# Forgetting attention: the row-maximum pass multiplies rounded copies of queries and keys

## The reference, cut to what matters

```python
q = rmsnorm(q.reshape(B, Lp, ATT_HEADS, ATT_HEAD_DIM), q_gain).transpose(0, 2, 1, 3)
k = rmsnorm(k.reshape(B, Lp, ATT_HEADS, ATT_HEAD_DIM), k_gain).transpose(0, 2, 1, 3)
logf = jax.nn.log_sigmoid(fl.astype(jnp.float32) + b_forget.astype(jnp.float32))
c = jnp.cumsum(logf, axis=1).transpose(0, 2, 1)
...
s = jnp.einsum('bhqd,bhkd->bhqk', q_i, k).astype(jnp.float32) * scale
s = s + c_i[..., :, None] - c[:, :, None, :]
mask = (pos[None, :] <= p_i[:, None]) & (pos[None, :] >= pad)
p = jax.nn.softmax(jnp.where(mask, s, NEG), axis=-1)
return jnp.einsum('bhqk,bhkd->bqhd', p.astype(v.dtype), v)
```

## Time and profile before

| | us |
|---|---|
| median of 3 runs | 2737.48 |
| lowest, highest | 2736.27, 2741.62 |
| span of the profiled execution | 2732.2 |
| TensorE busy in it | 2546.3 (93%) |
| VectorE, ScalarE, GpSimd busy | 1369.3, 973.2, 985.7 |
| forgetting attention, pairs 0 to 7 | from about 950 to 1300 |

### The profile page before, as it was taken

How to read it: one execution, slowest core, us unless ns; L and a number is a source line. 1 busy time by engine, 2 the same in 40 slices (tenths; PEclk the granted TensorE clock), 3 DMA queues, 4 the chain that set the end, 5 groups by cost and what they waited for, 6 DMA issues and landing times.

```text
span 2732.2 us, 45723 instructions
## 1 busy us (share of the span) xinstructions
PE 2546.3 (93%) x19794; PEld 2286.5 (84%) x19794; DVE 1369.3 (50%) x2057; ACT 973.2 (36%) x1565; POOL 985.7 (36%) x585
## 2 busy tenths in 40 slices
PE   7989978799999999999999999989998979999997
PEld 5877767678888888887999999988988968999997
DVE  4634455462635354444264554466654534727363
ACT  5234344232323444334433332354332224333232
POOL 1743344544444322222434444500002214445444
PEclk9999999999999999999999999999999988999998
DMA  9432120333332221111222332322111012233221
GB/s 248 121 94 63 53 70 24 92 96 97 93 93 87 68 55 47 40 47 40 78 62 85 89 90 85 87 59 70 40 33 36 17 32 59 85 92 87 87 87 60
DMA packets 379927, 201.33 MB, mean 74 GB/s; under 512 B 6464, under 2 KB 377152, under 8 KB 379728
## 3 DMA queue, kind: packets, MB, share of 16 engines
q1 hardware_dynamic: 379728, 198.42, 25.8%
HBM read 196.30 MB, written 2.10 MB: 73 GB/s over the span
## 4 chain that ended last, share of the span: by engine, by line
PE 57%; DVE 22%; ACT 11%; issue 4%; POOL 4%; DMA 1%; POOLq 0%; ACTq 0%; SPq 0%; DVEq 0%
PE ps L645 40%; DVE t_ffy L2829 7%; ACT t_wh L613 5%; DVE t_ffy L2832 2%; ACT t_ffy L2736 2%; DVE t_atq L2628 2%; POOL t_wl L623 1%; PE ps L2436 1%; DVE t_wl L623 1%; DVE t_ffy L2838 1%; PE ps L3061 1%; PE ps L2409 1%; PE ps L2375 1%; PE ps L3080 1%; PE ps L1090 1%
## 5 line engine op out<-in xcount | busy, mean ns | idle before, releaser
L623 POOL TENSOR_TENSOR t_wl<-t_raw,t_wh 128x1024 fp32r<-128x1024 f32 (+2 forms) x268 | 611.1, 2281 | 1030.1 <-ACT t_wh L613 1030.1
L613 ACT ACTIVATE t_wh<-t_raw 128x1024 fp32r<-128x1024 f32 (+2 forms) x323 | 327.7, 1015 | 605.8 <-PE ps L645 562.4
L645 PE MATMUL ps<-t_hh,t_wh 128*128 128x264 f32 (+2 forms) x2048 | 473.4, 310 | 14.4 <-DVE t_dcq L2562 3.6
L645 PE MATMUL ps<-t_hh,t_wl 128*128 128x264 f32 (+2 forms) x2048 | 449.4, 298 | 8.0 <-POOL t_wl L623 4.3
L645 PE MATMUL ps<-t_hl,t_wh 128*128 128x264 f32 (+2 forms) x2048 | 446.0, 299 | 0.0
L645 PEld LDWEIGHTS ps<-t_hh,t_wh 128*128 128x128 f32 x2048 | 323.7, 192 | 36.5 <-issue 17.6
L645 PEld LDWEIGHTS ps<-t_hh,t_wl 128*128 128x128 f32 x2048 | 324.0, 191 | 24.2 <-POOL t_wl L623 6.9
L645 PEld LDWEIGHTS ps<-t_hl,t_wh 128*128 128x128 f32 x2048 | 322.6, 191 | 9.1 <-issue 1.5
L645 PE MATMUL ps<-t_fhh,t_wh 128*128 128x264 f32 (+1 forms) x1040 | 280.9, 324 | 6.5 <-DVE t_fhl L1753 4.9
L645 PE MATMUL ps<-t_fhh,t_wl 128*128 128x264 f32 (+1 forms) x1040 | 281.5, 325 | 4.6 <-POOL t_wl L623 4.5
L2829 DVE SCALAR_TENSOR_TENSOR t_ffy<-t_ffp,t_vec,t_ffy 128x528 f32<-128x528 f32 x88 | 216.8, 2463 | 130.6 <-ACT t_ffy L2736 130.6
(11 more groups left out here) (558 smaller groups left out, 4351.3 us busy)
## 6 DMA issues: line engine op xcount, KB each, us to landing
t_raw<-in_up SPq DMA_DIRECT2D x44, 512.0 KB, 3.8
t_raw<-in_up2a SPq DMA_DIRECT2D x44, 512.0 KB, 3.9
t_raw<-in_up2b SPq DMA_DIRECT2D x44, 512.0 KB, 3.9
t_raw<-in_attn_in SPq DMA_DIRECT2D x33, 512.0 KB, 4.1
t_raw<-in_dn_in SPq DMA_DIRECT2D x33, 512.0 KB, 4.1
t_raw<-in_ada_w SPq DMA_DIRECT2D x32, 512.0 KB, 4.4
t_raw<-in_w_in SPq DMA_DIRECT2D x25, 512.0 KB, 4.4
t_raw<-in_down SPq DMA_DIRECT2D x16, 512.0 KB, 3.8
```

What stands on the lines that cost most here:

```text
L613: ac.activation(wh[slot_of[j]][:, 0:kc, :], raw[r % NRAW][:, 0:kc, :], ACT.Copy).then_inc(up("wh_cut", "cut", j), 1)
L623: eng.tensor_tensor(wl[slot_of[j]][:, 0:kc, :], raw[r % NRAW][:, 0:kc, :], wh[slot_of[j]][:, 0:kc, :].bitcast(F), SUB).then_inc(up(name, " ...
L645: ins = pe.matmul(ps[bank_of(j, i)][:, 0:tn], wt[slot][:, k, :], a[:, k, t0:t0 + tn], start=first, stop=last)
```

## The change

GpSimd gets a new kind of work, `round`: two copies of 128x528, the pair's normed queries and keys, into fp32r tiles (`t_aqr`, `t_akr`). It is put into the plan behind the pair's second `pair_norm`, but not before the pair ahead has put its six `row_max` steps, since the copies have one buffer (pair 0 has its own, in space of `t_apt`; pair 1's share space with `cT` and `aglog` and wait for their last readers). `row_max` multiplies the copies and waits for `rounded`; the wait for both norms moves to `weights`, which still multiplies `aq` and `ak` in fp32.

```diff
-        AFTER["pair_norm"] = lambda use, p, m: ready_qk.add((p, m))
+        rounded_at, maxima = [0], [0]
+
+        def put_round():
+            p = rounded_at[0]
+            if (p, 1) in ready_qk and p <= maxima[0]:
+                put("round", p)
+                rounded_at[0] += 1
+
+        def normed_pair(use, p, m):
+            ready_qk.add((p, m))
+            put_round()
+
+        AFTER["pair_norm"] = normed_pair
...
                     for i in range(6):
                         put("row_max", p, i, banks=2)
                         yield 1
+                    maxima[0] += 1
+                    put_round()
...
-                for m in range(2):
-                    w.wait_ge(s.normed, at("normed", "pair_norm", p, m))
+                w.wait_ge(s.rounded, at("rounded", "round", p))
...
-                    pe.matmul(ps[b][0:tn, 0:wide], aq[p % 3][64 * e:64 * e + 64, t0:t0 + tn],
-                              ak[p % 3][64 * e:64 * e + 64, a:a + wide], start=True, stop=False)
+                    qr, kr = (qround, kround) if p else (qround0, kround0)
+                    pe.matmul(ps[b][0:tn, 0:wide], qr[64 * e:64 * e + 64, t0:t0 + tn],
+                              kr[64 * e:64 * e + 64, a:a + wide], start=True, stop=False)
...
                 w.wait_ge(s.copied, at("copied", "turn_max", p))
+                for m in range(2):
+                    w.wait_ge(s.normed, at("normed", "pair_norm", p, m))
...
+            def round_(p):
+                for m in range(2):
+                    w.wait_ge(s.normed, at("normed", "pair_norm", p, m))
+                if p == 1:
+                    w.wait_ge(s.turned, at("turned", "split_c"))
+                    w.wait_ge(s.lo_dve, at("lo_dve", "split_c"))
+                elif p:
+                    w.wait_ge(s.scored, at("scored", "row_max", p - 1, 5))
+                qr, kr = (qround, kround) if p else (qround0, kround0)
+                po.tensor_copy(qr[:, :], aq[p % 3][:, :])
+                po.tensor_copy(kr[:, :], ak[p % 3][:, :]).then_inc(up("rounded", "round", p), 1)
```

More of the change, by code:

```diff
@@ L111 @@
     "lev_in lo_dve lo_pool mask_in maxed mm_done mod_mm mod_part mod_set multiplied normed out_d pool_step pool_x "
-    "rel_in rooted roped rstd_a rstd_d scaled scored sin_in sp_done sp_in sp_out spread sq_dve sq_pool "
+    "rel_in rooted roped rstd_a rstd_d scaled scored rounded sin_in sp_done sp_in sp_out spread sq_dve sq_pool "
     "squared step_x summed took_a took_d turned vec_in weighed wh_cut wl_dve wl_pool "
@@ L1849, in program @@
         sb_ = ExitStack()
+        with ExitStack() as st:
+            kround = sbt(st, "akr", [128, L], R)
         cT = sbt(sb_, "cT", [16, L])
@@ L1865, in program @@
         mrow = [sbt(sb_, f"amr{i}", [128, L], R) for i in range(2)]
+        with ExitStack() as st:
+            qround0, kround0 = sbt(st, "aqr0", [128, L], R), sbt(st, "akr0", [128, L], R)
         pT = [sbt(sb_, f"apt{i}", [128, 1360]) for i in range(2)]
         inv = sbt(sb_, "ainv", [128, L // 2])
+        with ExitStack() as st:
+            qround = sbt(st, "aqr", [128, L], R)
         glog = sbt(sb_, "aglog", [128, L])
@@ L2032, in program @@
             "pair_norm": "multiplied rooted inverted normed",
-            "values": "turned copied", "row_max": "scored maxed", "turn_max": "turned copied",
+            "values": "turned copied", "round": "rounded", "row_max": "scored maxed", "turn_max": "turned copied",
             "weights": "scored exped", "mixing": "weighed inverted scaled",
@@ L2694, in gated @@
                                  SUB).then_inc(up("lo_pool", "gated", pr), 1)
-            return {"gated": gated}
+            def round_(p):
[9 more added lines that the diff above has]
+                po.tensor_copy(kr[:, :], ak[p % 3][:, :]).then_inc(up("rounded", "round", p), 1)
+            return {"gated": gated, "round": round_}
         def stream_scalar(ac, w):
```

## The result

The changed kernel takes 2748.63 us (median of ten executions, 2741.7 to 2752.47) where the kernel before takes 2736.82 (2733.66 to 2741.73). The ratio is 1.004, 95% interval 1.003 to 1.005: 11.8 us, 0.43%. Timed a second time, in five rounds beside the kernel before (last experiment), it was 1.0039 (1.0024 to 1.0053), with 9.6 us between the medians. So it is slower by more than the 0.2% that can be told from no change.

A forecast was written before the change was run, and what follows sets the result against it. TensorE's columns were taken to bound the attention. Product gain -11.5, stalls +11.75, pair 0 +0.45 and clock +4.35 sum to +5.05 us; added to the median of 2737.48 this gave 2742.5 us, range 2733 to 2750.

The forecast's parts named there:

- Gain of the product: Row-maximum pass on TensorE: fp32r product saves 1.6 us a pair, 0.3 in pair 1, 11.5 us in total.
- Price of a cast: GpSimd's two new 128x528 casts per pair: 0.92 us each, the middle between 0.54 and 1.31.
- The queue and the stall: GpSimd's rounding holds a low half TensorE wants: five stalls of 2.55 us in pairs 3 to 7, 11.75 us lost net.
- 0.71 + 2T: TensorE's stall per pair in pairs 3 to 7, with T the time of one GpSimd cast: 2.55 us.
- T: Time of one 128x528 cast on GpSimd, taken as 0.92 us.
- the collision: Pair 7: VectorE's two-operand gating product slows beside GpSimd's held low halves, so 1.0 us comes back and not 1.43.
- The clock: TensorE's granted clock halves after three of the five stalls, 1.45 us each, 4.35 us in total.
- three drops: Half-clock pieces of about 3.4 us on TensorE after three of five stalls, 1.45 us each: 4.35 us.
- cheap-cast rival: Casts on GpSimd take 0.54 us, stalls 1.79 us, the clock holds: -3.5 us, 2734 us; chance 0.25.
- dear-cast rival: Casts on GpSimd take 1.31 us and the clock falls after every stall: +12.6 us, 2750 us; chance 0.19.
- harmless queue: Low half behind GpSimd's rounding isn't wanted so early, so the gain stays: some -11 us, 2726.5 us; chance 0.1.
- product without gain: Row-maximum product: 64 rows in fp32r run no faster than fp32, only losses stay, some +16.5 us; chance 0.01.

The follow-up runs named there:

- last experiment: The changed kernel, unaltered, timed again in five rounds beside the kernel before: 2745.77 us, ratio 1.0039.
- repeat of the late version: The changed kernel with each pair's rounding planned behind the low half of the panel two on, measured a second time on another chip: 2726.46 us, ratio 0.9968.
- late version: The changed kernel with each pair's rounding planned after the halves of the panel two on, not ahead of them: 2727.0 us, ratio 0.9955.
- pair-1 experiment: The late version with pair 1 alone multiplying its unrounded fp32 queries and keys: 2728.64 us, ratio 0.9958.

## Why the prediction was right, and where it was not

The time (2748.63) lies in the range of 2733 to 2750, near its upper end, and the sign was right; but the forecast said 2742.5, a change within 0.2%, and it is +0.43%. That the time lies in the range is in part luck, since two terms were wrong by several us in opposite directions. By its steps:

**Gain of the product: right.** 1.6 us a pair was forecast; pairs 2 and 6, which have no drop in their passes, are 1.68 us shorter, and the 400-column step takes the 0.55 us forecast. The 0.1 us taken off for exposed weight loads was not needed. For pair 1 I had left 0.3 us, for the same two reasons that the trace shows: the wait before step 4 (the steps counted from 0) grew by 0.85 us and step 5 waits 0.34 us for the same reductions. In the repeat of the late version, where the clock falls only behind this pass, it takes 10.71 us from its first step to its last mask and not 11.10, so the pair keeps 0.4. In all 12.2 us where I had 11.5.

**Price of a cast: wrong, and it helped the change.** I took the middle of 0.54 and 1.31 us, 0.92. It is 0.58 from start to start, close to the memset that only writes. Between two ends that lie far apart the middle had nothing for it. And there was a row of the same work, on another engine: the trace of before has a copy of 128x528 from fp32 into fp32r eight times on ScalarE, at 0.64 us (the line below). The Trainium skill (GPSIMD Engine Reference, Engine selection) had it: one-input operations run at roughly line rate, and the trace agrees with its 0.625 us for 528 columns. Pair 0 therefore cost nothing (0.45 forecast).

```profile
L2536 ACT ACTIVATE t_oh<-t_aog 128x528 fp32r<-128x528 f32 x8 | 5.2, 644 | 8.5 <-DVE t_aog L2665 8.5
```

**The queue and the stall: right in mechanism and place.** Five waits at L645 behind t_wl, in pairs 3 to 7 and nowhere else; with the measured 1.16 us for both casts the formula 0.71 + 2T gives 1.87 us, and 1.64 plus 0.2 of a slower start is 1.84. The late version removes all five, which shows the cause and doesn't only argue it. With T = 0.92 I had 11.75 us of stalls; it is 7.8. Pair 7 gave back its whole 1.43 us and not 1.0. VectorE's gating product in pair 7, beside the held low halves, took 1.27 us and not 1.03: the collision that I took from pair 0's 1.90 us is there, but cost little. In pair 0 itself it is as large as ever, 2.43 us for L1120 beside the low half; and in pair 2 it is the cast that takes 1.11 us instead of 0.62 beside that product, which itself takes 0.71, as good as the 0.70 before:

```profile
1035.95 0.62 POOL L2727 CAST t_aqr<-t_aq 128x528 fp32r<-128x528 f32 x1 [23.46 <-DVE t_ak L2653]
1036.51 1.11 POOL L2728 CAST t_akr<-t_ak 128x528 fp32r<-128x528 f32 x1
...
1036.42 0.71 DVE L2687 TENSOR_TENSOR t_aog<-t_aog,t_acc 128x528 f32<-128x528 f32 x1
...
965.81 2.43 DVE L1120 TENSOR_TENSOR t_asp<-t_asp,t_alf 128x80 f32<-128x80 f32 x1
```

**The clock: the step that failed.** I counted three drops, 4.35 us, tied them to waits of more than 2.5 us, and let the cheap-cast rival keep its clock because the earlier trace rows show 1.00 after a wait of 1.80 us. With cheap casts the waits were shorter than that, 1.64 us, and the stage had six, six, seven and nine drops, 8.7 to 13.1 us. Two things were missing: pair 1, whose longer wait brought one or two drops by itself, and drops that follow each other without a further wait. One case in which a wait had left the clock alone was no ground for a limit; the pair-1 experiment shows the same wait of 1.79 us with a drop. The price of a drop, 1.45 us, held: with it the parts add up to the stage within 0.8 us in twelve profiles with none to ten drops.

So the two errors had opposite signs: stalls 4 us too dear, the clock 4 to 9 us too cheap. The dear-cast rival gave 2750 us for a reason that wasn't there (its casts of 1.31 us) together with one that was (a clock that falls at nearly every wait). The harmless queue and the product without gain are refuted by the traces: five waits, and 0.55 us.

## What to carry to other kernels

A wait that is put into an in-order queue is paid for by whatever stands behind it: before moving small work to an idle engine, list the next entries of that queue and when each is wanted, and put the new work behind those wanted earlier than its own input is ready. Here the same sixteen casts made the kernel 0.3 to 0.45% faster (two runs) or 0.4% slower (two runs), by nothing but their place. And where TensorE is otherwise dense, count the clock with a new wait: here it cost about as much again as the wait itself. An experiment that fills the wait with products that nobody reads tells the two halves apart.

## What the runs showed of the hardware

A 128x528 copy from fp32 to fp32r takes 0.62 to 0.63 us on GpSimd, when nothing is in its way, and 0.63 to 0.65 on ScalarE, so the choice of engine was one of queues and not of speed. Filling a wait of 1.64 us with products that nobody reads kept the clock at 1.00 in all five places of the one profile taken, where in the four profiles of the changed kernel it fell in 13 of 20. And the length of a single wait doesn't tell what the clock does: after 1.64 us there were none to three drops at the same place of different executions, after 1.79 to 1.80 us three times none and once one, after 2.65 us one or two in ten profiles of ten.
